# The end of a 32-expert mixture: row buffers used in turn, a transpose moved ahead, and the token rows' adds moved from GpSimd to VectorE

## The reference, cut to what matters

```python
y = jnp.zeros_like(xt)
for e in range(N_EXPERTS):                       # 32
    he = jax.nn.silu(xt @ w_gate[e]) * (xt @ w_up[e])
    y = y + combine[:, e:e + 1] * (he @ w_down[e])
...
x = x + y.reshape(B, T, D)
return _rmsnorm(x, final_norm)
```

## Time and profile before

| | us |
|---|---|
| median of three executions | 1449.55 |
| lowest and highest of them | 1446.63, 1449.68 |
| the profiled execution, its own time | 1447.8 |
| its span in the profile | 1446.0 |
| mean granted clock of PE | 0.967 of full |

### The profile page before, as it was taken

The page is one execution under the profiler, slowest core; times in us unless marked ns, Lnnn a source line. Parts: engine busy times, 40 slices in busy tenths (PEclk is TensorE's granted clock), DMA queues, the critical chain, the costliest instruction groups (busy, mean ns, idle before and its releaser), DMA issues. The chain is left out here.

```text
span 1446.0 us, 20023 instructions
## 1 busy us (share of the span) xinstructions
PE 1329.0 (92%) x7696; PEld 950.5 (66%) x7696; DVE 666.5 (46%) x1346; ACT 505.5 (35%) x970; POOL 573.9 (40%) x531
## 2 busy tenths in 40 slices
PE   4999989989999899897998999999999889999985
PEld 3767767768878777565887877667767753333332
DVE  5456954257731679723772331534343621111116
ACT  3312333256632424334664232544442301111112
POOL 2113687334445336973346411544332321111125
PEclk8999999999999899999999999999999889999998
DMA  8772111130023311121002132221114949999984
GB/s 335 280 287 102 45 44 44 45 131 1 2 79 101 103 60 58 51 76 35 1 2 74 53 94 81 87 67 44 44 59 158 419 156 392 423 423 420 415 329 190
DMA packets 42652, 210.06 MB, mean 145 GB/s; under 512 B 7271, under 2 KB 9703, under 8 KB 33328
## 3 DMA queue, kind: packets, MB, share of 16 engines
q1 hardware_dynamic: 34336, 195.11, 35.3%
q0 software_dynamic: 5760, 10.27, 1.9%
q10 hardware_dynamic: 2448, 3.21, 0.8%
HBM read 201.98 MB, written 17.30 MB: 152 GB/s over the span
## 5 line engine op out<-in xcount | busy, mean ns | idle before, releaser
L425 POOL TENSOR_TENSOR wlo<-raw,whi 128x1024 fp32r<-128x1024 f32 x57 | 139.4, 2447 | 107.6 <-ACT whi L413 74.6
L3254 PE MATMUL ps<-gu,XT 128*64 128x512 f32 x608 | 136.5, 598 | 5.4 <-DVE XT L3352 3.4
L853 PE MATMUL ps<-hxh,whi 128*128 128x512 f32 x304 | 132.0, 434 | 5.5 <-ACT whi L413 5.5
L853 PE MATMUL ps<-hxh,wlo 128*128 128x512 f32 x304 | 124.5, 410 | 12.8 <-POOL wlo L425 12.8
L1115 DVE SCALAR_TENSOR_TENSOR z<-glu,small,z 128x798 f32<-128x798 f32 (+1 forms) x120 | 129.2, 1128 | 0.7
L853 PE MATMUL ps<-hxl,whi 128*128 128x512 f32 x304 | 123.3, 406 | 0.0
L3254 PEld LDWEIGHTS ps<-gu,XT 128*64 128x64 f32 x608 | 44.7, 137 | 84.2 <-issue 77.2
L1618 POOL TENSOR_SCALAR P<-P,stat 128x768 f32<-128x768 f32 (+1 forms) x80 | 65.8, 825 | 84.4 <-DVE stat L1580 83.2
L1462 PE MATMUL ps<-kT,qT 96*128 96x256 f32 (+1 forms) x432 | 91.9, 349 | 3.8 <-ACT P L1516 2.0
L1516 ACT ACTIVATE P<-ps,stat 128x768 f32<-128x768 f32 (+1 forms) x80 | 65.2, 815 | 63.2 <-DVE stat L1573 62.6
L853 PEld LDWEIGHTS ps<-hxh,wlo 128*128 128x128 f32 x304 | 59.4, 195 | 29.9 <-POOL wlo L425 16.0
(11 more groups left out here) (844 smaller groups left out, 3152.2 us busy)
## 6 DMA issues: line engine op xcount, KB each, us to landing
gu<-in_w_gu_dram SPq DMA_DIRECT2D x32, 2048.0 KB, 16.0
raw<-in_w_in_dram SPq DMA_DIRECT2D x66, 512.0 KB, 3.4
dn<-in_w_dn_dram SPq DMA_DIRECT2D x32, 1024.0 KB, 16.4
wgate<-in_w_mod_dram SPq DMA_DIRECT2D x16, 1024.0 KB, 9.0
raw<-in_w_out_dram SPq DMA_DIRECT2D x24, 512.0 KB, 3.3
wmod<-in_w_mod_dram SPq DMA_DIRECT2D x4, 2048.0 KB, 13.5
ybuf<-zero SPq DMA_DIRECT2D x1, 4096.0 KB, 12.1
yin<-ybuf SPq DMA_DIRECT2D x4, 1024.0 KB, 9.3
```

The costliest lines, as they stand in the source:

```text
L425: e.tensor_tensor(K.lo[i][:, :], K.raw[i % 2][:, :], K.hi[i][:, :].bitcast(F32), ALU.subtract).then_inc(*q.up("lo", i))
L853: p = e.matmul(s[0:m, o:o + n], a, K.h[l, v][x][:, k, :], start=k == 0 and part == 0 and x == 0, stop=end)
L3254: m = e.matmul(s[o, :], x[:, k, o], gu[:, k, :], start=k == 0, stop=k == KT - 1, skip_group_check=True)
```

## The change

Three things, all inside `experts_walk` and what it calls:

1. Pair `i`'s first pass uses `Y[i % 2]` and its second pass `Y[1 - i % 2]`; the scatters of first passes count on a semaphore of their own for each buffer.
2. After `down` of pair 14, `turn_up` of pair 15 comes at once, then `begin_sum(0)`, and only then the guarded second passes of pairs 14 and 15. These use a second buffer for their transposed rows, `heT2`, in a place of the weights that is free by then. `begin_sum(1)` moves behind `down` of pair 15, and `begin_sum`, `taken_in` and `finish` stand in another order from there on.
3. `rows_sum` on POOL goes. `take_in` on DVE is two adds of 128x1024, of the tokens' first and second rows, the second waiting for the first.

```diff
--- before.py
+++ after.py
@@ -2933,10 +2933,10 @@
     E.xg2, E.XT = sb("xg2_0", [128, D], F32, "xg2_"), sb("XT0", [128, KT, 128], F32, "XT")
     E.Y = [sb(f"Y{i}", [128, D], F32, "Y", 4096 * i) for i in range(2)]
     E.he = [sb(f"he{j}", [128, 256], F32, "he", 1024 * j) for j in range(3)]
-    E.heT = sb("heT", [128, 2, 128], F32, "he", 3072)
 
     last = NE - 6
     at = lambda w, x: f"{w}{x % (N_GU if w == 'gu' else N_DN)}"
+    E.heT = {"heT": sb("heT", [128, 2, 128], F32, "he", 3072), "heT2": sb("heT2", [128, 2, 128], F32, at("dn", last))}
     E.w_gu, E.w_dn = weight_place(K, "gu", last), weight_place(K, "dn", last)
     E.yin = [sb(f"yin{t}", [128, 2, D], F32, at("gu", last + t // 2), 8192 * (t % 2)) for t in range(T2)]
     E.parts = [[sb(f"y{j}{p}", [128, D], F32R, at("dn", (last + 1, last - 2)[j]), 4096 * c) for c, p in enumerate("hl")] for j in range(2)]
@@ -2958,6 +2958,11 @@
 def group_of(job):
     kind, n = job
     return GROUPS + n if kind == "far" else 2 * n + (kind == "second")
+
+
+def turned_of(E, job):
+
+    return E.heT["heT2" if job in (("second", PAIRS - 2), ("second", PAIRS - 1)) else "heT"]
 
 
 def weights_of(K, E, job):
@@ -3008,7 +3013,7 @@
 
 
 def experts_walk(S, engine, empty2=nothing, gather=nothing, load=nothing, turn_x=nothing, up=nothing, turn_up=nothing, down=nothing,
-                 scatter=nothing, stored=nothing, far_load=nothing, rows_in=nothing, owner=nothing, add=nothing, to_x=nothing, rows_sum=nothing,
+                 scatter=nothing, stored=nothing, far_load=nothing, rows_in=nothing, owner=nothing, add=nothing, to_x=nothing,
                  take_in=nothing, squares=nothing, finish_apart=nothing, finish=nothing):
 
     K, e = S.K, S.e
@@ -3037,11 +3042,11 @@
         up(job, xt, j, free(("he", j)))
         free.set(xt, ev("up", job))
 
-    def downward(job, j, y, part=None):
-        turn_up(job, j, free("heT"))
+    def downward(job, j, y, part=None, heT="heT"):
+        turn_up(job, j, free(heT))
         free.set(("he", j), ev("he_turned", job))
         down(job, y, part, free(("Y", y) if part is None else ("part", part)))
-        free.set("heT", ev("down", job, 1))
+        free.set(heT, ev("down", job, 1))
 
     def scattered(job, y):
         scatter(job, y, free(("Y", y)) if job[0] == "far" else [])
@@ -3054,7 +3059,7 @@
     def second_stored(i):
         def body():
             stored(("second", i))
-            free.set(("Y", 1), ev("stored", ("second", i)))
+            free.set(("Y", 1 - i % 2), ev("stored", ("second", i)))
         guarded(("pool",), crowded(i), body)
 
     def first_gather(i):
@@ -3070,12 +3075,12 @@
 
     def lower(i):
 
-        job, job2 = ("first", i), ("second", i)
-        down(job, 0, None, free(("Y", 0)))
+        job, job2, y = ("first", i), ("second", i), i % 2
+        down(job, y, None, free(("Y", y)))
         free.set("heT", ev("down", job, 1))
-        scattered(job, 0)
-        guarded(numbers, crowded(i), lambda: downward(job2, 1 + i % 2, 1))
-        guarded(("pool",), crowded(i), lambda: scattered(job2, 1))
+        scattered(job, y)
+        guarded(numbers, crowded(i), lambda: downward(job2, 1 + i % 2, 1 - y))
+        guarded(("pool",), crowded(i), lambda: scattered(job2, 1 - y))
         load(loads_of("dn", i))
     def far(n):
         job, y = ("far", n), n % 2
@@ -3131,7 +3136,7 @@
         owner(j, "dve", end)
         turned(job, "xg2", "XT")
         upward(job, "XT", 1)
-        downward(job, 1, None, 1)
+        downward(job, 1, None, 1, "heT2")
         for t in range(T2):
             for c in range(2):
                 add(job, j, 1, t, c, (ev("to_x", job, t, c), True, True))
@@ -3160,32 +3165,29 @@
     upward(("first", last), "XT", 0)
     down(("first", p), None, 0, free(("part", 0)))
     free.set("heT", ev("down", ("first", p), 1))
+    free.at["heT2"] = end
+    turn_up(("first", last), 0, free("heT"))
+    begin_sum(0)
     guarded(numbers, crowded(p), lambda: own_second(p, 1))
     second_gather(last)
     guarded(numbers, crowded(last), lambda: own_second(last, 3))
-    rows_sum(0)
     taken_in(0)
-    begin_sum(0)
-    begin_sum(1)
-    turn_up(("first", last), 0, free("heT"))
-    rows_sum(1)
     taken_in(1)
     down(("first", last), None, 1, free(("part", 1)))
-    rows_sum(2)
-    rows_sum(3)
+    begin_sum(1)
     begin_sum(2)
     end_sum(0)
     squares(0, x_of(0))
     finish_apart(0, x_of(0))
+    taken_in(2)
     end_sum(1)
     squares(1, x_of(1))
-    taken_in(2)
     begin_sum(3)
+    taken_in(3)
     end_sum(2)
     squares(2, x_of(2))
-    taken_in(3)
+    finish(1)
     end_sum(3)
-    finish(1)
     squares(3, x_of(3))
     finish(2)
     finish(3)
@@ -3274,7 +3276,7 @@
                     o = slice(n * i, n * i + n)
                     for w in q(ev("heT", job), loaded, *before):
                         e.wait_ge(*w)
-                    m = e.matmul(s[o, :], E.heT[:, k, o], dn[:, k, 512 * c:512 * c + 512], start=k == 0, stop=k == 1, skip_group_check=True)
+                    m = e.matmul(s[o, :], turned_of(E, job)[:, k, o], dn[:, k, 512 * c:512 * c + 512], start=k == 0, stop=k == 1, skip_group_check=True)
                     if k == 1 and i == len(ws) - 1:
                         m.then_inc(*q.up(*ev("down", job, c)))
 
@@ -3359,7 +3361,7 @@
     def turn_up(job, j, free):
         for w in q(ev("he_turned", job), *free):
             e.wait_ge(*w)
-        e.tensor_copy(E.heT[:, :, :], K.bank[ev("heT", job)][:, 0:256].rearrange("p (k q) -> p k q", q=128)).then_inc(*q.up(*ev("heT", job)))
+        e.tensor_copy(turned_of(E, job)[:, :, :], K.bank[ev("heT", job)][:, 0:256].rearrange("p (k q) -> p k q", q=128)).then_inc(*q.up(*ev("heT", job)))
 
     def down(job, y, part, free):
         g = group_of(job) if part is None else GROUPS - 4 + 2 * (job[1] - PAIRS + 2) + (job[0] == "second")
@@ -3388,9 +3390,10 @@
 
     def take_in(t, earlier):
         x = C.xN[:, t, :]
-        for w in q(("tail.rows", t), *earlier):
-            e.wait_ge(*w)
-        e.tensor_tensor(x, x, E.yin[t][:, 0, :], ALU.add).then_inc(*q.up("tail.taken", t))
+        for j, event in enumerate(("tail.rows", "tail.taken")):
+            for w in q(("yin", t), *(("tail.rows", t),) * j, *earlier):
+                e.wait_ge(*w)
+            e.tensor_tensor(x, x, E.yin[t][:, j, :], ALU.add).then_inc(*q.up(event, t))
 
     def finish(t):
         for w in q(("tail.root", t), ("row2",)):
@@ -3434,7 +3437,7 @@
     def scatter(job, y, free):
         g = group_of(job)
         event = ev("scatter", job)
-        done = q.land_as("y_out", *event) if job[0] == "first" else q.land_apart(f"second{event[1]}", *event)
+        done = q.land_as(f"y_out{y}", *event) if job[0] == "first" else q.land_apart(f"second{event[1]}", *event)
         for w in q(ev("y", job, 0), ev("y", job, 1), ("zero",), *free):
             e.wait_ge(*w)
         e.indirect_dma_start(out=K.ybuf, out_offset=bass.IndirectOffsetOnAxis(ap=E.row[:, g:g + 1], axis=0), in_=E.Y[y][:, :], in_offset=None,
@@ -3450,12 +3453,6 @@
         if engine == "pool":
             own_tokens(S, j, free)
 
-    def rows_sum(t):
-        y = E.yin[t]
-        for w in q(("yin", t)):
-            e.wait_ge(*w)
-        e.tensor_tensor(y[:, 0, :], y[:, 0, :], y[:, 1, :], ALU.add).then_inc(*q.up("tail.rows", t))
-
     def squares(t, ready):
         m = E.ms2[:, t:t + 1]
         for w in q(("tail.sq", t)):
@@ -3469,7 +3466,7 @@
         for w in q(("row2",), *ready):
             e.wait_ge(*w)
         e.tensor_tensor(E.yin[t][:, 1, :], C.xN[:, t, :], E.row2[:, :], ALU.mult).then_inc(*q.up("tail.weighted", t))
-    experts_walk(S, "pool", empty2=empty2, gather=gather, scatter=scatter, stored=stored, owner=owner, rows_sum=rows_sum, squares=squares, finish_apart=finish_apart)
+    experts_walk(S, "pool", empty2=empty2, gather=gather, scatter=scatter, stored=stored, owner=owner, squares=squares, finish_apart=finish_apart)
 
 
 
```

## The result

| | kernel before | changed kernel |
|---|---|---|
| median of 20 executions each, us | 1448.37 | 1451.41 |
| lowest and highest | 1445.70, 1450.45 | 1448.15, 1454.18 |
| ratio, 95% interval | | 1.0020, 1.0012 to 1.0027 |
| the profiled execution, its own time | 1447.8 | 1452.54 |
| its span | 1446.0 | 1450.7 |

The changed kernel is slower by about 3 us (1.7 to 3.9 by the interval), where the forecast had been 1.1 us faster.

A forecast was written before the change was run, and what follows sets the result against it. Weight transfers bound the kernel until 1400, then the wait for row buffer Y[0], then DVE from y0l on. 1.0 for row buffers plus 0.1 for DVE's end, taken from 1449.55, gave 1448.5 us; range 1445.2 to 1451.0.

The forecast's parts named there:

- Transpose ahead, sums later: PE's down of pair 15 starts about 1.1 us behind y0l instead of 3.9; 2.8 us off PE's chain, but DVE sets the time.
- Row buffers in turn: Pair 15's transposes start at 1399.0, its up at 1403.6, limited by the last gu; gain taken as 1.0 us.
- The clock: PE's low clock expected again until near 1407, so up of pair 15, 2.1 us earlier, saves 1.05; bounds 0.4 to 2.9.
- the first rival: PE's clock stays high around up of pair 15: 3.0 us gained, 1446.6, or 1445.3 with adds free of POOL; chance 17%.
- DVE's end, written out: DVE's instructions from y0l's end to its last, priced one by one: 24.3 us against 24.4 before.
- The third: DVE's adds of yin cost 3.1 us each whatever POOL does: 7.5 us more, 1456; chance 6%.
- The fourth: The change does nothing to the end, because PE's wait for the last gu is longer than read: 1449.5; chance 6%.
- The fifth: Weights aren't the bound; PE's 4.0 us come through whole with the clock high, if DVE follows: 1444.8; chance 5%.
- The second: The last gu comes 1.3 us late and PE's clock rises later: 1450.3, at worst 1451.2; chance 10%.
- my signs of being wrong: Pair 15's up before 1403 or 7.1 long, four adds over 5.5, or DVE waiting for yin or POOL's powers over 1 us.

The follow-up runs named there:

- experiment 2: Kernel before with only the new order and heT2, one row buffer and POOL's row sums kept: 1452.73 us, ratio 1.0025.
- experiment 8: Kernel before with begin_sum(0) alone moved ahead of the guarded second passes of pairs 14 and 15: 1452.68 us, ratio 1.0023.
- experiment 4: Changed kernel with pair 15's transpose and begin_sum(0) back behind the guarded second passes: 1447.56 us, ratio 0.9992 to the kernel before.
- 5: Changed kernel without the guarded second passes of pairs 14 and 15 and their branches: 1446.32 us, ratio 0.9982 to the kernel before.
- experiment 6: Changed kernel with the guarded second passes moved ahead of down of pair 14: 1446.85 us, ratio 0.9988 to the kernel before.
- 9: Changed kernel with begin_sum(0) alone back behind the guarded second passes, transpose still ahead: 1448.14 us, ratio 0.9992 to the kernel before.
- experiment 1: Kernel before with only the row buffers used in turn: 1445.48 us, ratio 0.9981.

## Why the prediction was wrong, by its own steps

*Transpose ahead, sums later* is the step that failed. It let `down` of pair 15 start 1.1 us behind `y0l` and run in 3.65, with the branches costed at 0.31 on DVE alone and at nothing on PE. What hid them before was never asked. In the changed kernel it started 1.56 behind `y0l`, and from there took 8.55: 1.90 for seven matmuls, 2.64 of hole, 4.01 for nine at the low clock. Against 1423.2 that is 0.46 for the late start, 0.30 in the seven, 2.64, and 4.01 - 9 x 0.228 = 1.96 for the clock, 5.4 in all; 5.0 of it reach DVE's end. Experiments 2 and 8 bring the loss back in the kernel before, 4, 5, 6 and 9 take it away. That the place of the branches, and the bodies behind them, are the cause is shown. That the stall is the fetch rests on the packets: in all three holes PE goes on 1.42 to 1.44 us after the packet's end. No run changed the fetch alone.

The Trainium skill (Runtime: NRT & Kernel Launch, "Instruction fetch mechanics") has a rule that the prediction left out: "A taken branch whose target isn't in the current 2-page window forces a DMA fetch of the target page before execution can continue". The trace agrees in part: a packet of 16 KB comes behind the branches, but PE ran seven matmuls before it stopped, so what was missing was code further on. The price is from the rows here: with the wait directly behind the branches 3.6 us of PE in the changed kernel, 2.0 in experiment 2 and 1.7 in experiment 8.

*Row buffers in turn:* right in kind, the term too small. I gave it 1.0; alone it gave 2.7, and its interval, 1.4 to 4.1, leaves 1.0 out. The transposes didn't start at 1399.0 but at 1402.8, behind the branch over the far passes. The sequencer's rows from 1390 to 1400 in the changed kernel show what I had not seen:

```profile
L2993 PEldq COMPARE_BRANCH  x2: 330/3994/7658, 1394.1 to 1394.6; - x2
```

The second branch stands for 7.66 us, until 1402.3. In the kernel before it stood 6.37 us, until 1400.2, under the longer wait for `Y[0]`. But the last `gu` was as late as that, so little was lost: `up` started 3.2 to 3.4 us earlier against the issue of `gu`, not 2.1. Of the difference 0.7 to 0.8 is `gu`, which took 16.0 and 15.9 instead of 16.7, and the rest is that `up` started 0.25 and 0.35 before it had landed: I had `up` wait for both experts' weights, but its first matmul needs only the first one's. DVE's end was 23.4 instead of 24.4 in experiment 1, since DVE's first add fell into the gap between POOL's first two row sums (1415.96 to 1417.33) and took 1.23 instead of 3.17. I had no term for that. It didn't come from earlier loads of `yin`: they were issued 1.0 us earlier than before, `y0l` ended 2.1 earlier.

*The clock:* not settled by one number. In the changed kernel the low level, 1.2 GHz, came again as forecast (0.58 from 1404 to 1408), and `up` of pair 15 took 8.92; in experiment 4 it took 9.00. In experiment 1 it didn't come there and `up` took 7.46, in experiment 6 it came and was all but gone when `up` began (7.38). That is 1.5 us between executions; my bounds had 0.8 for it, and the first rival's mechanism is what experiment 1 shows. One profile of each kernel can't say how often. A second fall, behind the hole, I had not thought of.

*DVE's end, written out:* 24.3 forecast, 24.3 in experiment 4, and 23.3 in experiments 5 and 6, where neither the guards on DVE nor PE's transpose stood between `y0l` and the adds. The 0.31 for guards didn't show in the changed kernel either, where DVE goes from `y0l` over the `heT` copy to the adds without a gap. In the changed kernel the end took 29.3, and the 5.0 more come from DVE's waits for what the late `down` gives it (2.30, 2.61 and 1.01), for which I had 0.2. Two adds took 2.47, not 2.56: the rule of the Trainium skill that a semaphore between them costs nothing (VectorE: DVE Perf Modes, "The DRAIN you can't avoid") was nearer than my 0.1. Tile 3's pair took 4.06 in the changed kernel beside POOL's scaling, so 1.6 more instead of 1.25.

*The rivals.* The third (adds dear by themselves) is refuted: four before 1424 took 4.88 together. The first came true in experiment 1, with part 1 alone (2.7 us measured against its 3.0); in the changed kernel the clock fell all the same. The fourth is out by experiment 1. The fifth is out too, since `up` came as the last `gu` landed (1404.60 against 1388.85 + 16.0 = 1404.85) and PE's 4 us didn't come through whole. The second was half true of the changed kernel (`gu` late, clock low) and isn't the cause. None of the five was the branches, and none of my signs of being wrong came either: `up` started after 1403, its matmuls took 8.92, four adds took 4.88, and DVE waited neither for `yin` nor for powers over 1 us. The sum of the three parts measured apart is about nothing (-2.7, +3.6, and -0.7 within the noise), the changed kernel is +3.0. With 1 to 1.5 us of uncertainty in each part that is hardly a contradiction; a reason could be that the branches meet the loads of `yin` more fully in the changed kernel (the hole is 1.6 us longer than in experiment 2), but that compares one execution of each. It stays open why the changed kernel's 20 times run from 1448.15 to 1454.18, wider than before's 1445.70 to 1450.45.

## What to carry to other kernels

A skipped body wasn't free here: behind the jump the engine needed code that had to be fetched, and that was hidden only where its sequencer got there early. The code also came latest where loads kept the transfer engines full. So before something that waits is moved ahead of a branch, read when the sequencer reaches the branch and what its slack is; move what doesn't wait, or move the branch ahead too. And when a wait is taken away, look at the engine's own sequencer for the next one.

## What the runs showed of the hardware

- PE's branch over the far passes stood 5.9 to 7.8 us in every kernel here; those over the second passes 0.23 to 0.37, but in the three kernels with `begin_sum(0)` directly ahead of them PE ran out of code a few matmuls further on.
- PE's sequencer is far ahead of the array when nothing holds it: in experiment 4 it was at the branches at 1414.2, the matmuls ahead of them ended at 1418.5. One matmul that waits for a semaphore takes that lead away: in the changed kernel it was there at 1418.7, behind the matmul that had waited for `y0l` (1418.51).
- The instruction packet of 16 KB behind the branches came later while the transfer engines were full: it started 2.6 to 3.4 us behind the branch beside the loads of `yin`, 0.3 to 0.4 without them.
- The hole of 2.64 us was followed by the lower clock (0.58 over the four us behind it), which cost nearly as much again (1.96). The one of 1.05 in experiment 2 left the clock at 1.00. But in experiment 8 it fell to 0.50 (1424 to 1426) behind a stop of only 0.85, so the length of one hole doesn't decide it.
